# Indexer head by head inside the qi, xr and gr tiles, gate, kv and q tiles ahead of ga, the output gate on the projected result, and a search word less

## The reference

```python
mod = silu(c) @ ada_w + ada_b;  shift, scale, gate = split(mod, 3)
h = rmsnorm(x, norm_g) * (1 + scale) + shift
z = h @ w_in
xr, gr, q, k, v, ga, qi, ki, wi = split(z)      # 512 512 512 64 64 512 512 64 8
xr = causal_depthwise_conv(xr)                  # width 4
y_r = rg_lru(xr) * silu(gr)                     # gates per 64-channel block, a scan over the rows
# indexer: score[t,s] = sum_h relu(qi[t,h] . ki[s] / 8) * wi[t,h] / sqrt(8), causal
# each row keeps its top 256 keys by score; masked softmax attention, 8 heads of 64, shared k and v
y_a = attention(q, k, v, top256(score)) * silu(ga)
y = concat(y_r, y_a) @ w_out
out = rmsnorm(x + gate * y, final_g)
```

## Time and profile before

| what | value |
|---|---|
| median of 3 runs | 681.26 us (681.05 to 681.62) |
| the profiled execution | 682.19 us |
| its span, first to last instruction | 680.4 us |
| TensorE matmuls busy | 557.4 us, 82% |
| VectorE busy | 450.7 us, 66% |
| ScalarE busy | 386.6 us, 57% |
| GpSimd busy | 244.6 us, 36% |
| mean granted TensorE clock | 0.902 |
| HBM, mean over the span | 62 GB/s |

### The profile page before, as it was taken

The page is one execution under the profiler, slowest core; times in us unless marked ns, Lnnn a source line. Parts: engine busy times, 40 slices in busy tenths (PEclk is TensorE's granted clock), DMA queues, the critical chain, the costliest instruction groups (busy, mean ns, idle before and its releaser), DMA issues.

```text
span 680.4 us, 8136 instructions
## 1 busy us (share of the span) xinstructions
PE 557.4 (82%) x2704; PEld 453.4 (67%) x2704; DVE 450.7 (66%) x1021; ACT 386.6 (57%) x693; POOL 244.6 (36%) x201
## 2 busy tenths in 40 slices
PE   2379999888799369491799997276999999999995
PEld 2356888656678247181676885266889998888874
DVE  5984000877995998959699796467566666655631
ACT  6423122585459589496789365343465666666631
POOL 5042656063425353445472553454120202022121
PEclk9759999998999779596799999555999999999999
DMA  8940446200101011026112322800201001010111
GB/s 341 409 118 1 120 129 145 72 31 0 32 1 51 11 32 31 3 82 255 32 32 62 92 65 63 285 24 1 93 16 47 30 34 53 11 63 30 35 62 63
DMA packets 15450, 51.98 MB, mean 76 GB/s; under 512 B 3888, under 2 KB 3888, under 8 KB 14384
## 3 DMA queue, kind: packets, MB, share of 16 engines
q1 hardware_dynamic: 15408, 51.45, 23.5%
HBM read 37.81 MB, written 4.19 MB: 62 GB/s over the span
## 4 chain that ended last, share of the span: by engine, by line
PE 51%; DVE 19%; ACT 12%; issue 8%; DMA 5%; POOL 2%; SPq 2%; DVEq 0%; POOLq 0%; ACTq 0%
PE pair L1272 16%; PE pair L1381 13%; PE pair L1403 6%; PE pair L1414 5%; DMA ada<-in_ada_w 4%; ACT bias_sb L779 3%; DVE bias_sb L1013 3%; PE pair L1359 3%; PE pair L1360 2%; PE pair L1266 2%; PE pair L1423 2%; DVE score_sb L1130 2%; DVE tinies L1029 1%; DVE rnn_xc L1102 1%; ACT relu L793 1%
## 5 line engine op out<-in xcount | busy, mean ns | idle before, releaser
L1272 PE MATMUL pair<-h_hi,w_hi 128*128 128x512 f32 (+1 forms) x352 | 113.4, 404 | 20.8 <-ACT raw L756 17.7
L1272 PE MATMUL pair<-h_hi,w_lo 128*128 128x512 f32 (+1 forms) x352 | 110.3, 395 | 0.0
L1272 PE MATMUL pair<-h_lo,w_hi 128*128 128x512 f32 (+1 forms) x352 | 110.1, 394 | 0.0
L779 ACT ACTIVATE bias_sb<-score_sb,tinies 128x1024 bf16<-128x1024 f32 (+2 forms) x93 | 95.7, 1031 | 21.2 <-DVE tinies L1029 21.1
L1203 DVE TENSOR_TENSOR pt_lo<-pair,pt_hi 128x512 fp32r<-128x512 f32 (+3 forms) x96 | 50.5, 554 | 64.7 <-ACT pt_hi L884 64.3
L1272 PEld LDWEIGHTS pair<-h_hi,w_hi 128*128 128x128 f32 (+1 forms) x352 | 65.5, 190 | 38.1 <-issue 24.3
L1272 PEld LDWEIGHTS pair<-h_lo,w_hi 128*128 128x128 f32 (+1 forms) x352 | 66.3, 188 | 15.5 <-issue 0.8
L1272 PEld LDWEIGHTS pair<-h_hi,w_lo 128*128 128x128 f32 (+1 forms) x352 | 66.2, 188 | 15.2 <-issue 0.4
L1013 DVE TENSOR_SCALAR_CACHE_REDUCE bias_sb<-score_sb,tinies 128x640 bf16<-128x640 f32 (+2 forms) x93 | 74.0, 796 | 0.0
L884 ACT ACTIVATE pt_hi<-pair 128x512 fp32r<-128x512 f32 (+3 forms) x96 | 43.6, 489 | 27.6 <-PE pair L1414 25.3
L591 POOL TENSOR_SCALAR w_hi<-w_raw 128x1024 fp32r<-128x1024 f32 (+1 forms) x22 | 25.7, 1166 | 89.9 <-PE pair L1272 74.0
(11 more groups left out here) (200 smaller groups left out, 1378.4 us busy)
## 6 DMA issues: line engine op xcount, KB each, us to landing
w_raw<-in_w_tiles SPq DMA_DIRECT2D x21, 512.0 KB, 3.9
ada<-in_ada_w SPq DMA_DIRECT2D x8, 1024.0 KB, 18.9
x_sb<-in_x SPq DMA_DIRECT2D x8, 512.0 KB, 7.6
qs<-half_hi SPq DMA_DIRECT2D x16, 256.0 KB, 3.6
qs<-half_lo SPq DMA_DIRECT2D x16, 256.0 KB, 4.4
ada_g<-in_ada_w SPq DMA_DIRECT2D x1, 4096.0 KB, 13.7
wo_raw<-in_w_out SPq DMA_DIRECT2D x8, 512.0 KB, 7.4
x_res<-in_x SPq DMA_DIRECT2D x8, 512.0 KB, 3.3
```

Source lines behind the costliest of these rows:

```text
L779: nc.scalar.activation(junk[i], score_sb[:, SCORE_OFF[i]:SCORE_OFF[i] + keys_of(i)], ACT.Sign, bias=cand[:, c:c + 1], scale=-1.0, accum_ou ...
L1272: ins = nc.tensor.matmul(psum[banks[half]][0:width, :], w[b][:, k, 0:width], hh[:, k, half * HALF:(half + 1) * HALF], start=(k == 0 and p ...
```

## The change

- The tiles go in a new order: behind gr 3 come gate, kv, q 0 to 3, and all four ga tiles last. The list `ORDER` now starts at qi 1.
- The indexer's units go head by head over all six blocks. They stand between the k-steps of qi 2, qi 3, xr 0 and gr 0, 12 units a tile. The causal fills and the sign counts (`nonneg`) of all six come behind the last unit.
- `stages()` books loads of VectorE and ScalarE, and spaces the search rounds by 4 us and what else falls due in the round. The conv and recurrence steps have slightly other due times.
- A search round keeps no spare word: the candidate becomes candidate xor miss xor half the bit.
- `w_out` isn't multiplied by the gate. VectorE multiplies each projected half by the gate into `yg`, and GpSimd adds it to x; for the last row block VectorE adds. The high half of `w_out` is made in steps 5 to 12. TensorE waits for `y_ok` where it waited for `x1_ok`.
- Output pieces start at step 20, two a step for seven steps.
- `fg_bc` and `yg` lie in freed columns of `qs`; `fg_bc` is loaded behind the 16th attention score.
- VectorE no longer waits for all ga tiles ahead of attention (a later wait is kept); TensorE waits for the last eviction only at step 1. `ada_g` is loaded behind the indexer, `gate_b` at the gate tile.

By the list made from the new durations, rounds 26 to 30, `post`, and all compares and masks stand behind the eviction of ga 3; round 0 stands between `decay` and `root` of group 0; rounds 1 and 2 stand ahead of `gates` of group 1, rounds 3 and 4 ahead of group 2's, 5 and 6 ahead of group 3's.

```diff
-TILES += [("ga", _ct, P) for _ct in range(3)]
-TILES += [("kv", 0, P), ("gate", 0, P)] + [("q", p, P) for p in range(4)] + [("ga", 3, P)]
+TILES += [("gate", 0, P), ("kv", 0, P)] + [("q", p, P) for p in range(4)] + [("ga", p, P) for p in range(4)]
...
-UNITS = [(i, h) for a, b in PAIRS for h in range(NH) for i in (a, b)]
+UNITS = [(i, h) for h in range(NH) for a, b in PAIRS for i in (a, b)]
...
+WO_START = 5
+OUT_START = 20
...
+HEAD_UNITS = 2 * len(PICK)
...
-    ks = [(j, k) for j in range(J["xr", 0], NJ) for k in range(KC)]
+
+    ks = [(j, k) for j in range(J["qi", 1], NJ) for k in range(KC)]
...
+        n = j - J["qi", 2]
+        if 0 <= n < 4:
+            for _ in range(HEAD_UNITS * (k + 1) // KC - HEAD_UNITS * k // KC):
+                w = keys_of(UNITS[units][0])
+                at(now, "idx", units, dve=0.2 + w / 900, act=0.2 + w / 1200)
+                now += 2 * w / 2400 + 0.06
+                units += 1
+            if units == len(UNITS) and not start:
+                at(now + 2.0, "causal")
+                for c in range(len(PICK)):
+                    at(now + 3.0, "nonneg", c, dve=0.9)
+                at(now + 4.0, "bias01")
+                at(now + 8.0, "prep", dve=3.0)
+                at(now + 9.0, "sign", act=3.0)
+                start = now + 12.0
...
-            if kind == "ga" and ct == 0:
+            if kind not in ("qi", "xr", "gr"):
                 us = max(us, rnn_us)
-            at(us, "evac", j)
+            if (kind, ct) == ("q", 0):
+                us += 2 * 1.365
...
+    t = start
     for it in range(SEARCH_BITS):
-        at(start + 4.0 + ROUND_US * it, "count", it)
-    end = start + 4.0 + ROUND_US * SEARCH_BITS
-    at(end, "post")
+        at(t, "count", it)
+        end = t + ROUND_US
+        for _ in range(3):
+            d, a = (sum(x[n] for x in load if t <= x[0] < end) for n in (1, 2))
+            end = t + ROUND_US + max(d, a)
+        t = end
...
-                if kind == "ga" and n == 1:
-
-                    sp.wait_ge(slot_done, len(SLOT))
+                if kind == "xr" and n == 1:
+
+                    sp.wait_ge(slot_done, IDX_SLOTS)
                     sp.dma_start(ada_g[:, :, :], ada_w[:, 2 * D:3 * D].rearrange("(k p) n -> p k n", p=P)
                                  ).then_inc(adag_in, 16)
+                if kind == "gate":
...
+            sp.wait_ge(ga_ok, 4)
             for ti in range(2):
                 sp.dma_start(x_res[ti][:, :], x[ATT[ti] * P:(ATT[ti] + 1) * P, :]).then_inc(xres_in[ti], 16)
+
+            sp.wait_ge(att_ps, 16)
+            sp.dma_start(fg_bc, final_g.rearrange("(a c q) -> a c q", a=1, q=P).partition_broadcast(P)).then_inc(fg_in, 16)
...
+                if ti < NT - 1:
+                    pool.wait_ge(xres_in[ti % 2], 16 * (ti // 2 + 1))
+                    for half in range(2):
+                        pool.wait_ge(y_ok, 2 * ti + half + 1)
+                        xs = x_res[ti % 2][:, half * HALF:(half + 1) * HALF].rearrange("p (c q) -> p c q", q=P)
+                        nc.gpsimd.tensor_tensor(xs, yg[half], xs, ALU.add).then_inc(x1_ok, 1)
...
-                def narrow(c, hits):
-                    dve.wait_ge(hit_ok, 4 * it + hits)
-                    nc.vector.tensor_tensor(icand[:, c:c + 1], cols(c, hit), cols(c, spare[it % 2]), ALU.bitwise_xor).then_inc(cand_a, 1)
+                    nc.vector.tensor_scalar(cols(c, miss), cols(c, cnt), cols(c, lim), float(bit), ALU.is_gt, ALU.mult).then_inc(miss_ok, 1)
+
+                def narrow(c, misses):
+                    dve.wait_ge(miss_ok, 4 * it + misses)
+                    nc.vector.scalar_tensor_tensor(icand[:, c:c + 1], cols(c, miss), bit >> 1, icand[:, c:c + 1],
+                                                   ALU.bitwise_xor, ALU.bitwise_xor).then_inc(cand_a, 1)
...
-                if it < SEARCH_BITS - 1:
-                    nc.vector.scalar_tensor_tensor(spare[1 - it % 2][:, :], hit[:, :], flip, spare[it % 2][:, :], ALU.bitwise_xor, ALU.bitwise_xor).then_inc(spare_ok, 1)
...
-            dve.wait_ge(ga_ok, 4)
...
-                if g % 2 == 0 and g < 16:
-
-                    m = g // 2
-                    dve.wait_ge(gate_ok, 1)
+                if WO_START <= g < WO_START + KC:
+
+                    m = g - WO_START
                     dve.wait_ge(wo_in[m], 16)
-                    nc.vector.tensor_tensor(wo_raw[:, m, :], wo_raw[:, m, :], gate_bc[:, :], ALU.mult).then_inc(wo_scaled, 1)
-                if g % 2 == 1 and g < 16:
-                    m = g // 2
-                    dve.wait_ge(wo_scaled, m + 1)
                     nc.vector.tensor_scalar(wo_hi[:, m, :], wo_raw[:, m, :], 1.0, None, ALU.mult).then_inc(wo_hi_ok, 1)
                 for o in PIECES.get(g, ()):
                     if o % 4 != 3:
                         continue
                     ti, half = divmod(o // 4, 2)
                     dve.wait_ge(out_ps, 2 * ti + half + 1)
-                    if half == 0:
-                        dve.wait_ge(xres_in[ti % 2], 16 * (ti // 2 + 1))
-                    xs = x_res[ti % 2][:, half * HALF:(half + 1) * HALF]
-                    nc.vector.tensor_tensor(xs, bank(3), xs, ALU.add).then_inc(x1_ok, 1)
+                    if ti + half == 0:
+                        dve.wait_ge(gate_ok, 1)
+                    if ti:
+                        dve.wait_ge(x1_ok, 2 * (ti - 1) + half + 1)
+                    nc.vector.tensor_tensor(yg[half], bank(3).rearrange("p (c q) -> p c q", q=P),
+                                            gate_bc[:, half * HALF:(half + 1) * HALF].rearrange("p (c q) -> p c q", q=P), ALU.mult).then_inc(y_ok, 1)
+                    if ti == NT - 1:
+                        if half == 0:
+                            dve.wait_ge(xres_in[ti % 2], 16 * (ti // 2 + 1))
+                        dve.wait_ge(y_ok, 2 * ti + half + 1)
+                        xs = x_res[ti % 2][:, half * HALF:(half + 1) * HALF].rearrange("p (c q) -> p c q", q=P)
+                        nc.vector.tensor_tensor(xs, yg[half], xs, ALU.add).then_inc(x1_last, 1)
...
-                            pe.wait_ge(x1_ok, 2 * ti + half)
+                            pe.wait_ge(y_ok, 2 * ti + half)
...
+                    if g == LAG_T:
+                        pe.wait_ge(evac_done, NJ)
```

More of the change, by code:

```diff
@@ L115, in stages, with at @@
     due = []
-    def at(us, *what):
+    load = []
+    def at(us, *what, dve=0.0, act=0.0):
         due.append((us, len(due), what))
-    ks = [(j, k) for j in range(J["xr", 0], NJ) for k in range(KC)]
+        load.append((us, dve, act))
+    ks = [(j, k) for j in range(J["qi", 1], NJ) for k in range(KC)]
     now = 0.0
@@ L124, in stages @@
     rnn_us = 0.0
-    for n, (j, k) in enumerate(ks):
+    start = 0.0
+    for j, k in ks:
         kind, ct, _ = TILES[j]
@@ L152, in stages @@
                 for t in range(CONV):
-                    at(now + 1.5 + 1.3 * t, "conv", ct, t)
+                    at(now + 1.5 + 1.3 * t, "conv", ct, t, dve=1.3)
             if kind == "gr":
-                gates.append((now + 0.5, ct))
-        if IDX_FIRST <= n + 1 <= IDX_FIRST + IDX_OVER:
-            upto = len(UNITS) * (n + 1 - IDX_FIRST) // IDX_OVER
-            while units < upto:
-                at(now, "idx", units)
-                now += 2 * keys_of(UNITS[units][0]) / 2400 + 0.06
-                units += 1
-                if units % (2 * NH) == 0:
-                    p = units // (2 * NH) - 1
-                    at(now + 2.0, "causal", p)
-                    for i in PAIRS[p]:
-                        at(now + 3.0, "nonneg", PICK.index(i))
-                if units == len(UNITS):
-                    start = now + 5.0
-    at(start - 2.0, "bias01")
-    at(start, "prep")
-    at(start + 2.0, "sign")
-    for it in range(SEARCH_BITS):
-        at(start + 4.0 + ROUND_US * it, "count", it)
-    end = start + 4.0 + ROUND_US * SEARCH_BITS
-    at(end, "post")
+                gates.append((now + 4 * 1.36, ct))
+    t = start
+    for it in range(SEARCH_BITS):
+        at(t, "count", it)
[4 more added lines that the diff above has]
+        t = end
+    at(t, "post")
     for c in range(len(PICK)):
-        at(end + 4.0 + 4.4 * c, "cmp", c)
-        at(end + 6.6 + 4.4 * c, "mask", c)
-        at(end + 10.9 + 4.4 * c, "bias", c)
+        at(t + 4.0 + 4.4 * c, "cmp", c)
+        at(t + 6.6 + 4.4 * c, "mask", c)
+        at(t + 10.9 + 4.4 * c, "bias", c)
     return [what for _, _, what in sorted(due)]
@@ L361, in layer_kernel @@
         pick = tiny(6)
-        hit = tiny(6, I32)
-        spare = [tiny(6, I32) for _ in range(2)]
+        miss = tiny(6, I32)
         negmax = tiny(3)
```

90 lines of the change are left out of this document (44 added, 46 removed).

## The result

| what | before | after |
|---|---|---|
| median | 681.44 us (681.05 to 681.62, 4 runs) | **692.25 us** (691.94 to 693.14, 4 runs) |
| ratio, 95% interval | | 1.0161 [1.0144, 1.0179] |
| span of the profiled execution | 680.4 us | 690.2 us |
| mean granted TensorE clock | 0.902 | 0.898 |

The change is slower by 10.8 us. The forecast was 677.3 with a range of 661 to 691, so the time lies 1.2 us above its upper end. It went the way of rival A, which was priced at 691.

A forecast was written before the change was run, and what follows sets the result against it. The prediction took the projections to end last ahead of attention, hiding the search, with matmuls binding 500 to 650. Span 680.4 + 0 - 7 + 3 = 676.4, execution 678.2, median 677.3 us; range 661 to 691.

The forecast's parts named there:

- rival A: Recurrence cycle with in-order ScalarE takes 36.5 us, not 32; three cycles add 13.5 ahead of q 0: 691 us, chance 0.25.
- Part 1: Indexer head by head, in four tiles between qi 2 and gr 0: done at 158.3 us.
- Part 2: From the indexer's end to the projections' end: one gr buffer paces the loop, and TensorE ends ga 3 at 384 us.
- the cycle of the recurrence: Loop over channel groups ahead of q 0: summed durations plus 0.8 for hand-overs give 32 us a cycle.
- Rival B: Recurrence loop near 27 us by better overlap of GpSimd and VectorE with the rounds: 663 us, chance 0.17.
- one buffer: Recurrence: gr c+1's eviction waits for yr of c, in-order ScalarE stands still; TensorE waits some 14 us at q 0.
- Part 3: Behind the last tile: five rounds, settle and masks put the first exponential at 434.3 us against 434.47, change 0.
- Part 4: Gate on the result, w_out loads, ga wait: -7 us in the first 16 attention steps, +3 in return.
- fit the same gaps: Copies to wo_hi, one a step from step 5, fit the gaps left by the removed multiplies in early attention.
- The return: Output multiplies and adds, last-tile adds, pieces from step 20 and ScalarE waits cost +3 us (0 to +7).
- One sign of being wrong: The forecast is wrong if the stage from step 20 on is longer than before by over 7 us.
- Part 5: Search without the spare word: rounds run at ScalarE's 3.1 us, change 0 (at most -2.5).

The follow-up runs named there:

- e1: Kernel after, with GpSimd's slab split behind a gr tile (groups 1 to 3) moved behind yr of the group before: 686.79 us.
- e2: Kernel after, with two buffers for the evicted gr, so an eviction waits for yr of two groups back: 670.35 us.
- e3: Kernel after, with ScalarE making the high half of w_out ahead of the first compare, in place of VectorE: 688.75 us.
- e7: Kernel after, with ScalarE making the high half of w_out and output pieces from step 17 instead of 20: 687.60 us.

## Why the prediction was wrong

**Part 1 was right.** The last relu ends at 158.25 (158.3 forecast). Part 2 begins near its forecast too: round 0 starts at 176.73 (178), and gr 1 is evicted by 202.6 (201). In between, two conv steps of the first cycle took 5.3 us, beside GpSimd, where undisturbed ones take 1.28 each.

**The step that failed is the cycle of the recurrence in Part 2, "0.8 for hand-overs: 32".** It measured 35.7 and 36.2. By its terms, from the silu load at 205.65: up to GpSimd's first instruction 17.6 us, where my terms less the round sum to 18.8. GpSimd's 1 - th and product took 5.2, not 3.1; they ran beside two conv steps, and in the third cycle, without conv steps beside it, the product took 2.34 of the 3.30. From the product's end to the start of `yr` it was 6.4, where I had the scan's 2.3 alone, because a slab split of 6.4 stood between the two in GpSimd's list (3.6 where VectorE did not run beside it). `yr` took 2.4 and not 2.9; the eviction of gr and the round behind it took the 4.1 forecast, without the 0.8 for hand-overs. I had the slab split nowhere in the sum: I read the order of ScalarE's steps from `stages()`, but not what GpSimd's own list held between `pool_rnn` 1 and 2. e1 shows that without it the cycle is 32.7 and 33.2, near the forecast, and in part by luck: the stretched product is paid for by terms that I had taken too long. The third cycle, from the eviction of gr 3 to that of the gate tile, took 29.1, forecast 29; the gate tile was evicted at 303.6 and not 294. From there to the end of the projections it took 89.8 us, forecast 90, with a wait ahead of q 0 of 14.7 (14). Of the 9.4 us by which the projections are late, 7.9 come from the two long cycles, and 1.6 were there when gr 1 was evicted.

**Rival A was this case, and underweighted.** Its cycle of 36.5 and time of 691 are nearly what happened, the time in part by luck: A put 13.5 us on three cycles, where two cycles were long and the projections came 9.4 late, and the misses of Part 4 made up for it. I had given it 0.25 because 44.3 in the kernel before held seven rounds. The rows showed stretched steps and I had used them for the tail and for `yr` only.

**Rival B did not happen, but its cycle is reachable.** Its 27 us is what the second buffer gives (24.0 and 27.0, e2), though not by the better overlap that B had. The forecast had the right cause of the wait, "one buffer".

**Part 3 was right.** The tail is 48.8, forecast 50.3 (434.3 less 384), with the five rounds in it. The masks ran at their short rows (20.7 us, 21.3 forecast), with GpSimd idle: on 896 keys the step that took 2.00 in the earlier trace rows took 1.15.

**Part 4 was mis-sized.** The first 16 steps got 2.5 us shorter, not 7. With the multiplies and the copies both off VectorE the steps take 31.5 us, 7.5 less than before (e3, e7); what the multiplies alone are worth, with the copies left in every second step, no run shows. But that the copies "fit the same gaps" was wrong: one a step, they take turns with GpSimd's subtractions at 2.98 us each, 5.0 us on the path. The return was +4.6 for a forecast of +3. Of it 2.8 are the pieces from step 20 (e7), for which I had 1.6. The stretch behind step 60 cost 1.6, of which 0.7 is the added second row at the end, as forecast; the other 0.9 stays open. VectorE's timeline of the kernel after:

```profile
682.95 0.69 DVE L1205 TENSOR_TENSOR q_free<-pair,gate_bc 128x512 f32<-128x512 f32 x1 [4.87 <-PE pair L1404]
683.67 0.69 DVE L1212 TENSOR_TENSOR x_res<-q_free,x_res 128x512 f32<-128x512 f32 x1
```

One sign of being wrong came up: from step 20 to the end it took 197.6 us, 10.2 more than before (187.3), and the sign stood at 7. It was badly chosen: 5.6 of the 10.2 only moved, because steps 16 to 19 got that much shorter (14.0 for 19.6 us) when their output pieces went behind step 20.

**Part 5 was right.** Rounds without other work between them still start 3.07 to 3.15 us apart.

**The sum of the misses**, on the span: Part 2 +9.4, tail -1.5, first steps +4.5, the return +1.6, together +14.0. Between the spans it is 13.8 (690.2 less 676.4); the other 0.2 is the 434.3 that the forecast had taken as no change from 434.47. The range missed by 1.2 us because A was priced by itself, with Part 4 at its middle. In both errors VectorE and GpSimd hold each other up, which is why they may fall on the same side. A range for that case should have joined them.

## What to carry to other kernels

When a change makes a loop the bound, write down each engine's own list within one cycle, not only the order of the engine that waits; a foreign step between producer and consumer stands in the cycle unless the consumer would have waited anyway (here the split of 6.4 us cost 3.0). Look for the single buffer in such a loop first: here one more buffer of 4 KB a partition was worth 22 us in the new order and nothing in the old. A gain in front of a hidden tail is only as large as the tail lets through, so plan both together.
